# Feed-forward up projections of the second block: seven products for more pairs of weight blocks, one weight sum on GpSimd

## The reference, cut to what matters

```python
def conv_glu_ffn(x, w_up, conv_w, conv_b, w_down):
    u = x @ w_up                       # x: tokens x 1024, u: tokens x 5632
    u = causal_depthwise_conv(u, conv_w, width=3) + conv_b
    gate, val = jnp.split(u, 2, axis=-1)
    return (jax.nn.silu(gate) * val) @ w_down
h = h + conv_glu_ffn(rms_norm(h, norm_ffn_g), ...)
```

## Time and profile before

| | |
|---|---|
| runs | 1408.86, 1406.27, 1406.71 us, median 1406.71 |
| profiled execution | 1400.61 us, of which span 1398.8 us |
| TensorE busy | 1370.2 us (98%), granted clock 0.995 |
| VectorE busy | 912.0 us (65%) |
| ScalarE busy | 319.7 us (23%) |
| GpSimd busy | 26.6 us (2%) |

### The profile page before, as it was taken

How to read it: one execution, slowest core, us unless ns; L and a number is a source line. 1 busy time by engine, 2 the same in 40 slices (tenths; PEclk the granted TensorE clock), 3 DMA queues, 4 the chain that set the end, 5 groups by cost and what they waited for, 6 DMA issues and landing times.

```text
span 1398.8 us, 28132 instructions
## 1 busy us (share of the span) xinstructions
PE 1370.2 (98%) x11816; PEld 1262.3 (90%) x11816; DVE 912.0 (65%) x1820; ACT 319.7 (23%) x667; POOL 26.6 (2%) x32
## 2 busy tenths in 40 slices
PE   9999999999999999998998999999999999999997
PEld 8899888999999987977897998999999779999997
DVE  3288433347885547677654878787676557878865
ACT  2134203250000121331232222221111433222211
POOL 0140000000001000000000000000000000000000
PEclk9999999999999999999999999999999999999999
DMA  9444344247445432431000444444545214544551
GB/s 369 161 149 153 106 166 150 76 152 233 171 161 181 156 117 76 136 106 47 3 4 9 136 136 166 138 168 162 181 151 170 69 50 140 177 157 145 167 188 68
DMA packets 57127, 190.63 MB, mean 136 GB/s; under 512 B 9232, under 2 KB 11536, under 8 KB 56752
## 3 DMA queue, kind: packets, MB, share of 16 engines
q1 hardware_dynamic: 50768, 180.93, 37.7%
q10 hardware_dynamic: 6240, 7.97, 1.8%
HBM read 187.82 MB, written 1.05 MB: 135 GB/s over the span
## 4 chain that ended last, share of the span: by engine, by line
PE 94%; DVE 3%; ACT 1%; issue 1%; DMA 0%; ACTq 0%; DVEq 0%; PEldq 0%
PE ps L1971 92%; PE ps L936 2%; DMA arena<-in_x_t 0%; DVE arena L1781 0%; DVE arena L1788 0%; ACT arena L1376 0%; DVE rs L2456 0%; PE ps L999 0%; PE ps L1199 0%; ACT arena L2404 0%; ACT arena L1370 0%; DVE arena L1793 0%; DVE arena L1906 0%; DVE arena L1729 0%; ACT arena L1468 0%
## 5 line engine op out<-in xcount | busy, mean ns | idle before, releaser
L1971 PE MATMUL ps<-arena,ring 128*128 128x128 f32 (+6 forms) x4720 | 800.7, 321 | 2.4 <-PEq L836 0.8
L1971 PEld LDWEIGHTS ps<-arena,ring 128*128 128x128 f32 x4720 | 703.3, 191 | 69.1 <-issue 7.8
L1971 PE MATMUL ps<-arena 128*128 128x128 f32 (+10 forms) x5414 | 548.6, 267 | 7.6 <-ACT arena L1376 2.2
L1971 PEld LDWEIGHTS ps<-arena 128*128 128x128 f32 (+3 forms) x5414 | 498.0, 174 | 29.9 <-issue 12.7
L895 DVE TENSOR_TENSOR arena<-ring 128x512 f32<-128x512 f32 x104 | 71.8, 690 | 119.5 <-PE ps L1971 84.8
L882 ACT COPY arena<-ps 128x128 f32<-128x128 f32 (+2 forms) x76 | 20.3, 267 | 352.5 <-PE ps L1971 352.5
L1755 DVE SCALAR_TENSOR_TENSOR arena<-arena,cols 128x271 f32<-128x271 f32 (+3 forms) x176 | 82.9, 492 | 9.8 <-ACT arena L1345 6.7
L1345 ACT ACTIVATE arena<-arena,cols 128x272 f32<-128x272 f32 (+1 forms) x88 | 48.8, 601 | 122.8 <-DVE arena L1683 68.9
L897 DVE TENSOR_TENSOR arena<-arena,ring 128x512 f32<-128x512 f32 x104 | 72.4, 696 | 3.6
L900 DVE TENSOR_TENSOR arena<-ring,arena 128x512 f32<-128x512 f32 x104 | 72.2, 694 | 0.0
L898 DVE TENSOR_TENSOR arena<-ring 128x512 f32<-128x512 f32 x104 | 71.4, 686 | 0.0
(11 more groups left out here) (284 smaller groups left out, 907.2 us busy)
## 6 DMA issues: line engine op xcount, KB each, us to landing
ring<-in_stream SPq DMA_DIRECT2D x342, 512.0 KB, 3.8
consts<-in_consts ACTq DMA_DIRECT2D x1, 1420.0 KB, 12.7
arena<-in_mem_t ACTq DMA_DIRECT2D x1, 1024.0 KB, 7.3
res<-in_x_t ACTq DMA_DIRECT2D x1, 1024.0 KB, 18.6
out_t<-arena SPq DMA_DIRECT2D x4, 256.0 KB, 2.5
arena<-in_x_t ACTq DMA_DIRECT2D x3, 256.0 KB, 5.1
arena<-in_g ACTq DMA_DIRECT2D x1, 640.0 KB, 6.6
arena<-in_w ACTq DMA_DIRECT2D x2, 256.0 KB, 5.0
```

The lines of the kernel that those rows point to most:

```text
L1971: return nc.tensor.matmul(out, lhs, rhs, start=start, stop=stop)
```

## The change

It makes 19 pairs of each layer seven-product pairs: m = 1, 3, 5 and every m from 6 to 21. Pairs 6, 8, ..., 20, eight in each layer, were plain before. All 19 use a new order and placing:

```diff
-("ffa_up", Seven(..., WIDE, 1, F2, GB, True, 2), 1),
+("ffa_up", Seven(..., CHAIN, 1, F2, GB, True, CHAINED), 2),
+CHAIN_ORDER = (1, 5, 2, 6, 4, 7, 3)
+CHAIN = {4: (0, 0), 2: (0, 1), 5: (0, 2), 1: (1, 0), 6: (1, 0), 7: (1, 0), 3: (2, 0)}
+SCALED_FROM = 6
+CHAINED = (1, 3, 5) + tuple(range(SCALED_FROM, F2))
```

Products 1, 6 and 7 add up in one PSUM region. ACT copies it after each of them, and TensorE waits for the copy before it adds the next:

```diff
+for p in order_of if y.chained else ():
+    if p in (5, 6, 3):
+        pe.wait_ge(w_summed, done + {5: 1, 6: 2, 3: 4}[p])
+    if p == 6:
+        pe.wait_ge(p1_kept, y.pair(i) + 1)
+    if p == 7:
+        pe.wait_ge(third_summed, y.chain0 + y.nth(i) + 1)
+        pe.wait_ge(partial_kept, 2 * (y.chain0 + y.nth(i)) + 1)
...
+    if p in (1, 6, 7):
+        last.then_inc(products, 1)
```

ACT's queue for each m, with the copies of the next pair around the work of this one:

```diff
 for m in range(F2):
-    if m % 2:
-        keep_first_product(act, name + "_up", m)
+    if m + 1 in CHAINED:
+        keep_first_product(act, name + "_up", m + 1)
     ... two Identity activations of m ...
+    if m + 1 in CHAINED:
+        keep_partial_sum(act, name + "_up", m + 1, 2)
     ... Silu of m ...
+    if m + 1 in CHAINED:
+        keep_partial_sum(act, name + "_up", m + 1, 3)
```

The weight sum s3 leaves DVE for the end of POOL's program; s2 and s4 stay, s4 now behind a wait for s2:

```diff
+def third_weight_sums(pool, name):
+    for i in y.pairs():
+        arrived(pool, b)
+        arrived(pool, b + 1)
+        pool.wait_ge(used, y.block(y.two_before(i) + 1) if y.nth(i) >= 2 else y.first)
+        nc.gpsimd.tensor_tensor(WSUM[name][y.group(i, 0) % 2][:, 2], a11, a21, ALU.subtract
+                                ).then_inc(third_summed, 1)
```

DVE's take-out shrinks from five additions and a scaling to three additions; for m below 6 the scaling stays:

```diff
+def quads_chained(name, i, dst):
+    dve.wait_ge(products, 3 * y.pair(i) + 3)
+    dve.wait_ge(partial_kept, 2 * (y.chain0 + y.nth(i)) + 1)
+    link(tt(quarters[:, 2:4, :], q[:, 0:2, 0:y.t], <products 2 and 5>, ALU.add))
+    dve.wait_ge(used, y.block(i + 1))
+    link(tt(quarters[:, 3, :], quarters[:, 3, :], product_at(y, i, 3), ALU.add))
+    dve.wait_ge(partial_kept, 2 * (y.chain0 + y.nth(i)) + 2)
+    last = tt(quarters[:, 0:2, :], over(q[:, 2, 0:y.t], 2), <products 4 and 5>, ALU.add)
+    if i < SCALED_FROM:
+        link(last)
+        last = tt(dst, dst, over(rs[:, 0:2 * y.t], 2), ALU.mult)
+    last.then_inc(ev[name], 2)
```

(The second operands above are cut short to the regions that they read.) Instead, DVE scales the input once, and makes its sums, in time for pair 6; and weight sums of m + 2 are made in every turn whose m + 2 is seven-product:

```diff
+if m + 2 in CHAINED:
+    weight_sums(dve, tt, up, m + 2, 0)
+if m == 2:
+    for j in range(4):
+        last = tt(hf_scaled[name][:, 2 * j:2 * j + 2, :], hf[:, 2 * j:2 * j + 2, tokens(name)],
+                  over(rs[:, 0:width], 2), ALU.mult)
+    link(last)
+if m == 4:
+    x_sums(link, tt, up, scaled=True)
```

More of the change, by code:

```diff
@@ L178 @@
     own: bool
-    step: int = 1
+    chained: tuple = ()
+    chain0: int = 0
     pair0: int = 0
@@ L187, in pair, with nth, two_before @@
     def pair(self, i):
-        return self.pair0 + (i - self.i0) // self.step
+        return self.pair0 + self.nth(i)
     def group(self, i, g):
-        return self.group0 + len(self.groups) * ((i - self.i0) // self.step) + g
+        return self.group0 + len(self.groups) * self.nth(i) + g
     def pairs(self):
-        return range(self.i0, self.n, self.step)
+        return self.chained or range(self.i0, self.n)
+    def nth(self, i):
+        return self.chained.index(i) if self.chained else i - self.i0
+    def two_before(self, i):
+        return (self.chained[self.nth(i) - 2] if self.nth(i) >= 2 else -1) if self.chained else i - 2
     def turn(self, i):
-        return i // self.step % 2
+        return self.nth(i) % 2 if self.chained else i % 2
     def taken(self, i):
-        return self.off + 2 * (i - 2 * self.step + 1)
+        return self.off + 2 * (self.two_before(i) + 1)
 class Space:
@@ L505, in program @@
             XSUM[name], WSUM[name], QUADS[name] = square_x[name == "sb_q"], square_w, square_q
+        at += 8 * T2
+        hf_scaled = {"ffa": arena[:, at:at + KT * L].rearrange("p (n t) -> p n t", n=KT),
+                     "ffb": arena[:, at:at + KT * L2].rearrange("p (n t) -> p n t", n=KT)}
+        SCALED = {name + "_up": x.rearrange("p (k b) t -> p k b t", b=2) for name, x in hf_scaled.items()}
+        at += KT * L
+        XSUM_SCALED = [arena[:, at + n * 4 * T2:at + (n + 1) * 4 * T2].rearrange("p (k t) -> p k t", k=4)
+                       for n in range(4)]
+        assert at + 16 * T2 <= width
+        partial_kept, third_summed = sem("partial_sums_kept"), sem("third_weights_summed")
         SRC["gate"] = SRC["upq"] = h.rearrange("p (k b) t -> p k b t", b=2)
@@ L843, in seven_products @@
             y = SEVEN[name]
-            b11, b12, b21, b22 = x_quarters(name)
-            t1, t2, t3, t4 = x_summed_quarters(name)
+            scaled = bool(y.chained) and only >= SCALED_FROM
+            b11, b12, b21, b22 = x_quarters(name, scaled)
+            t1, t2, t3, t4 = x_summed_quarters(name, scaled)
             x_of = {1: b11, 2: b21, 3: b22, 4: t4, 5: t1, 6: t2, 7: t3}
-            lead, end = [{y.place[p][0]: p for p in order} for order in (ORDER[::-1], ORDER)]
+            order_of = CHAIN_ORDER if y.chained else ORDER
+            lead, end = [{y.place[p][0]: p for p in order} for order in (order_of[::-1], order_of)]
+            if scaled and only == SCALED_FROM:
+                pe.wait_ge(x_summed, y.sums0 + 3)
             for i in y.pairs() if only is None else (only,):
@@ L864, in seven_products @@
                                                         "sb_q": 2}.get(name, 1))
-                    for p in ORDER:
+                    for p in order_of if y.chained else ():
[6 more added lines that the diff above has]
+                            pe.wait_ge(partial_kept, 2 * (y.chain0 + y.nth(i)) + 1)
+                        for l in range(n):
+                            last = nc.tensor.matmul(product_at(y, i, p), w_of[p][:, l, :], x_of[p][:, l, :],
+                                                    start=l == 0 and p == lead[y.place[p][0]],
+                                                    stop=l == n - 1 and (p in (1, 6) or p == end[y.place[p][0]]),
+                                                    skip_group_check=p in (6, 7))
+                        if p in (1, 6, 7):
+                            last.then_inc(products, 1)
+                    for p in () if y.chained else order_of:
                         if p in (6, 7, 3):
@@ L878, in keep_first_product @@
             y = SEVEN[name]
-            act.wait_ge(products, 3 * y.pair(i) + (3 if y.place[2][0] == y.place[1][0] else 1))
+            act.wait_ge(products, 3 * y.pair(i) + (3 if y.place[2][0] == y.place[1][0] and not y.chained else 1))
             if y.taken(i) > 0:
@@ L882, in keep_first_product, with keep_partial_sum @@
             nc.scalar.copy(QUADS[name][y.turn(i)][:, 0, 0:y.t], product_at(y, i, 1)).then_inc(p1_kept, 1)
+        def keep_partial_sum(act, name, i, n):
+            y = SEVEN[name]
+            act.wait_ge(products, 3 * y.pair(i) + n)
+            nc.scalar.copy(QUADS[name][y.turn(i)][:, n - 1, 0:y.t], product_at(y, i, 1)).then_inc(partial_kept, 1)
+        def third_weight_sums(pool, name):
+            y = SEVEN[name]
+            for i in y.pairs():
+                b = y.block(i)
+                a11, a12, a21, a22 = w_quarters(b)
+                arrived(pool, b)
[3 more added lines that the diff above has]
+                                        ).then_inc(third_summed, 1)
         def weight_sums(dve, tt, name, i, g):
@@ L890, in weight_sums @@
             arrived(dve, b + 1)
-            if y.step == 1 and (b - 4 >= y.block(y.i0) or not y.own):
+            if not y.chained and (b - 4 >= y.block(y.i0) or not y.own):
                 dve.wait_ge(used, b - 2)
-            elif i >= y.i0 + 2 * y.step:
-                dve.wait_ge(used, y.block(i - 2 * y.step + 1))
+            elif y.chained and y.nth(i) >= 2:
+                dve.wait_ge(used, y.block(y.two_before(i) + 1))
             tt(s1, a21, a22, ALU.add).then_inc(w_summed, 1)
@@ L897, in weight_sums, with x_sums @@
             tt(s2, s1, a11, ALU.subtract).then_inc(w_summed, 1)
-            tt(s3, a11, a21, ALU.subtract).then_inc(w_summed, 1)
+            if not y.chained:
+                tt(s3, a11, a21, ALU.subtract).then_inc(w_summed, 1)
             dve.wait_ge(w_summed, done + 2)
[L900 to L904, removed]
+            tt(s4, a12, s2, ALU.subtract).then_inc(w_summed, 2 if y.chained else 1)
+        def x_sums(link, tt, name, at=slice(None), scaled=False):
+            b11, b12, b21, b22 = [x[:, at, :] for x in x_quarters(name, scaled)]
+            t1, t2, t3, t4 = [x[:, at, :] for x in x_summed_quarters(name, scaled)]
             link(tt(t1, b12, b11, ALU.subtract))
@@ L1787, in first @@
                 for half in range(2):
-                    tt(tmt[c][HALF[half], :].rearrange("p (i a j) -> p i a j", i=KT // 2, a=2),
+                    last = tt(tmt[c][HALF[half], :].rearrange("p (i a j) -> p i a j", i=KT // 2, a=2),
                        head_rows_of(gram[c], half, half)[:, :, :, 0:CH],
                        const("pairs")[HALF[half], :].rearrange("p (i a j) -> p i a j", i=1, a=1).to_broadcast(
```

(6 more changed lines are left out.)

35 lines of the change are left out of this document (20 added, 15 removed).

## The result

The changed kernel takes 1420.22 us (median of 5) against 1406.61 us for the kernel before on the same chip: ratio 1.0091, interval 1.0070 to 1.0112. It is slower by 13.6 us in the medians and lies above the forecast's 1411.5 us and the range's upper end, 1418; the direction was forecast, the size was not (+5). Its profiled execution took 1416.55 us, 15.9 us over the one of before.

What follows compares the result with a forecast made beforehand. VectorE with collisions was taken as the bound after the change: +0.3 in ffa, +3.1 in ffb, +3.6 start, -1 per layer, together +5 us on the 1406.71 median, about 1411.5 us; 8-in-10 range 1395.5 to 1418.

Steps and rivals of the forecast that it cites:

- What bounds the kernel: Up stages: TensorE sets the pace before the change, busy 14 of 14 us; VectorE, with collisions, after it.
- Removed from TensorE, 12.8 us: Up stages: eight pairs per layer become seven-product, saving 6.7 us in ffa and 6.1 us in ffb.
- The mechanism and its price: Up stages: GpSimd's subtraction and VectorE's two-input SBUF operations exclude each other, costing VectorE 0.94 us in every turn.
- How late may VectorE be: Up stages: product 7 waits for ACT's partial-sum copy behind VectorE's take-out; VectorE may be 2.2 us late.
- The sum: Both up stages: +0.3 us in ffa, +3.1 in ffb, +3.6 for the start, -1 per layer at the end; together +5 us.
- The turn: VectorE's loop in ffa: 5.58 us without collision plus 0.94 us for it, before input sums.
- The last turn: End of each up stage: not charged, since no pair follows; -1 us per layer.
- the start: Turns 3, 4 and 5 of each layer: lateness passes the slack by about 1.8 us, +3.6 us; 0 to 4 in the range.
- Gain kept: Up stages: GpSimd's operation falls into PSUM additions or gaps, TensorE stays the bound; 1395.7 us, chance 0.22.
- Half of it: Up stages: VectorE gets back in step in ffa only, or half the turns collide; some -6 us, 1400.7 us, chance 0.17.
- ACT's or DMA's order: Up stages: late weight blocks or copies behind Silu add a wait of their own; above 1420 us, chance 0.05.
- The chunk stage at nothing: Chunk stage: the `first_part` wait becomes a chained one, costing nothing.

Runs made afterwards that it cites:

- experiment 2: The changed kernel without any third weight sum, product 7 taking s2 as weights (other numbers result): 1390.46 us, ratio 0.9891 to the kernel before.
- experiment 3: The changed kernel with GpSimd's sum released when VectorE begins its take-out, the first two pairs' after the layer's input sums: 1392.79 us, ratio 0.9916.
- experiment 5: The changed kernel with only the third sums of each layer's first two pairs released later, after the layer's input sums: 1416.34 us, ratio 1.0091 to before.
- experiment 4: The kernel before with only the chunk stage's wait changed as in the change: 1406.58 us, ratio 1.0005.
- experiment 7: The changed kernel with GpSimd making 256 of 512 columns of each third sum, s2 giving product 7's other weights: 1396.69 us, ratio 0.9946 to before.

## Why the prediction was right or wrong

**What bounds the kernel**: right. TensorE before, VectorE after, with the pair periods of a turn of VectorE's loop.

**Removed from TensorE, 12.8 us**: right as a price; the pairs of experiments 2 and 3 are 6.49 and 6.25 us apart. By the marks these two get back 10.2 and 9.8 us of it. Of the 2.6 us that experiment 2 lacks, 1.8 are the waits at the start of the layers (0.8 in each, and 0.2); the last 0.8 stays open.

**The mechanism and its price**: right. 0.94 us was taken, and 0.95 was paid in 29 turns. The 0.94 was the middle between two bounds, 0.83 and 1.06; that it hit within 0.01 us is luck. The operation's length is that of the earlier trace rows: GpSimd's subtraction takes 1.27 us undisturbed in experiment 3, not the 1.04 of the earlier trace rows. By the Trainium skill's "GPSIMD Engine Reference", section 4.1, it would have been an estimated 1.38; the rows are nearer. That nearly every turn pays was right too: from pair 6 on, 13 of 16 in each layer do, and the last three have no sum of GpSimd's beside them.

**How late may VectorE be**: right. The wait on the partial sum's copy is where TensorE stands, five times in each layer and up to 1.8 us. At pair 6 it is 1.73 and 1.79 us, where about 1.8 was worked out; 0.8 of that is there without collisions too (experiment 2).

**The sum** is the step that failed: it said +5, and the two up stages cost +13.9. The mechanism held, but one term was too small, one was missing, and one was a credit that the runs don't show:

- *The turn*, 6.52 us, measured 6.65. A linked operation waits for the one before it. I counted the 0.72 us of such a step from s2 to s4; it measured 0.80, though s2 behind s1, with the same kind of wait, still takes 0.71. The third addition starts 0.38 us after the second instead of 0.33. Why these two steps are longer, no run shows. The product's step is 1.32 (0.36 + 0.96) instead of 1.30, and 1.42 where input sums follow, since they wait for the product. With that turn it is 7.10 per pair instead of 6.93, and 7.00 instead of 6.82 in ffb: 16 x 0.17 + 16 x 0.18 = 5.6 us.
- *GpSimd's sums of the first two pairs* weren't counted at all; I took their release, which waits for nothing in the layer, as harmless. They run at the end of the stage before and the start of this one, where VectorE's additions and input sums hold up TensorE: 2.4 us (experiment 5).
- *The last turn*, taken as -1 us per layer since no pair follows. TensorE still waits 0.76 and 0.85 us at product 7 of pair 21. What the other two terms leave open is 13.9 - 5 - 5.6 - 2.4 = 0.9 us, less than the credit of 2; that it is this term's is an inference from the remainder.

The range was too narrow at its dear end for that reason: it let the price of a collision and the start vary, but held the turn of 5.58 us without collision fixed, and the measured 1420.22 us lie 2.2 above 1418.

**Rivals.** *Gain kept* didn't happen, but its place was right: experiment 3 makes it happen by moving the release into the PSUM additions. *Half of it* didn't happen either: in both layers alike 13 of 16 turns paid. *ACT's or DMA's order* didn't decide: experiment 2 has the same order in ACT's queue and waits 0.8 us per layer.

**The chunk stage at nothing**: right (experiment 4 and the marks).

## What to carry to other kernels

Work given to an idle GpSimd isn't free if it reads SBUF: a subtraction of 1.27 us stopped a VectorE operation with two SBUF operands for 0.95 us here. It belongs beside VectorE's PSUM operations, and releasing it there by VectorE's own progress instead of TensorE's was worth 26 us in this kernel. When an engine's cover shrinks to a few per cent, take the distance of each pair of dependent operations from a row of just that pair (0.80 us here where 0.72 was taken from another), and follow every instruction of a moved chain, the first ones included, into the stage where it will run.

## What the runs showed of the hardware that was not expected

GpSimd's 128x512 subtraction took 1.27 us in nearly every turn of experiment 3, where nothing held it up, but in the changed kernel VectorE lost only 0.95 of it. One part of the difference is at the end: a product that takes 0.44 us ended at 873.68 where GpSimd's operation ended at 873.39, so by its usual length it resumed at 873.24, 0.15 us before that end. The rest is at the front: GpSimd's operation, 1.43 us long here, had begun 0.33 us before the product (1.43 - 0.33 - 0.15 = 0.95).

Executions of one and the same kernel lie at two levels by their granted clock. Of the kernel before, those with a mean of 0.994 to 0.997 took 1400.2 to 1402.6 us, those with 0.990 to 0.992 took 1405.7 to 1409.1. Of the changed kernel, two runs at 0.995 took 1415.3 and 1416.6 us and three at 0.991 to 0.992 took 1420.2 to 1420.5, so it is 11 to 16 us slower at either level. Where the lower level arises, the profile of experiment 7 (0.991) shows: between 760 and 780 us its granted clock was 0.66, where the profile of before has 1.00, and its mark before ffa lies at 800.9 us instead of 794.5. In the 20 us ahead TensorE had been busy for 17.4 us in the one and 17.3 in the other, so these rows don't tell why one was throttled and the other not. Medians of a few runs hold some of that: experiments 2 and 3 differ by 2.3 us in their medians but by 0.1 us in their profiled executions (1390.70 and 1390.59 us, both at 0.995).
